# One instruction for the maxima of both attention maps of a block of queries

## What is computed

```python
h = rms_norm(x, norm_pre) * (1.0 + scale) + shift          # scale, shift, gate from c @ ada_w
q, k, v, z = (h @ w_in[:, i * 2048:(i + 1) * 2048] for i in range(4))
# 8 heads, two maps (m = 0, 1) of 128 features each, v of 256 features
for each block of 128 queries:
    sc = einsum('bqhmd,bkhmd->bhmqk', q, k) * scale
    p = softmax(where(mask, sc, NEG_INF))                  # causal by chunks of 64
    attn = p[:, :, 0] - lam * p[:, :, 1]
    o = attn @ v
o = rms_norm(o, subln) * 0.8 * silu(z)
out = x + gate * rms_norm(o @ w_out, norm_post)
```

## Time and profile before

| | us |
|---|---|
| median of three runs | 2067.22 (2063.76 to 2068.3) |
| the profiled execution | 2068.47 |
| its span | 2066.7 |
| busy: TensorE, VectorE, ScalarE, GpSimd | 1981.3, 1295.6, 785.1, 580.9 |
| seven heads beside the input products | about 826 to 1665 in the span |

### The profile page before, as it was taken

One profiled execution on the slowest core, in us unless ns is written; L12 is line 12 of the kernel. 1 busy time (PEld: TensorE's weight loads), 2 busy tenths in 40 slices (PEclk: granted clock), 3 DMA queues, 4 the chain that ended last, 5 costly groups with the idle time before them and its releaser, 6 DMA issues.

```text
span 2066.7 us, 26660 instructions
## 1 busy us (share of the span) xinstructions
PE 1981.3 (96%) x9324; PEld 1610.8 (78%) x9324; DVE 1295.6 (63%) x1988; ACT 785.1 (38%) x1567; POOL 580.9 (28%) x640
## 2 busy tenths in 40 slices
PE   3689999999999989999999999999999989999998
PEld 1168888888888878788888888888888878888886
DVE  3766676666566436777777777777777745434343
ACT  4333333333454323344444444444444333322240
POOL 2333233233456224232332333233232210000000
PEclk9889999999999999999999999999999999999999
DMA  9657666663556586776758676676767685476552
GB/s 311 198 183 244 221 199 207 200 197 124 175 183 227 211 325 219 207 236 195 233 178 248 196 216 216 209 236 200 234 193 237 196 275 165 123 229 199 178 153 82
DMA packets 391489, 426.52 MB, mean 206 GB/s; under 512 B 21078, under 2 KB 287420, under 8 KB 388796
## 3 DMA queue, kind: packets, MB, share of 16 engines
q1 hardware_dynamic: 391072, 424.76, 65.1%
q10 hardware_dynamic: 284, 0.05, 0.0%
HBM read 294.70 MB, written 130.03 MB: 206 GB/s over the span
## 4 chain that ended last, share of the span: by engine, by line
PE 90%; DMA 2%; DVE 2%; issue 2%; POOL 1%; ACT 1%; SPq 1%; DVEq 0%; POOLq 0%; ACTq 0%
PE ps L1561 28%; PE ps L1563 27%; PE ps L1562 27%; PE ps L1667 2%; PE ps L1675 2%; PE ps L1645 1%; DVE acc L1146 1%; PE ps L1541 1%; SPq L475 1%; PE ps L1694 1%; POOL sums L727 1%; POOL stg L747 1%; DMA h_dr<-stg 1%; DVE blk L1175 0%; DMA w_raw<-in_diff_w_out_dram 0%
## 5 line engine op out<-in xcount | busy, mean ns | idle before, releaser
L1561 PE MATMUL ps<-blk,ring 128*128 128x512 f32 x1536 | 612.4, 399 | 12.6 <-POOL blk L738 5.9
L1563 PE MATMUL ps<-blk,ring 128*128 128x512 f32 x1536 | 600.9, 391 | 0.0
L1562 PE MATMUL ps<-blk,ring 128*128 128x512 f32 x1536 | 600.4, 391 | 0.0
L1561 PEld LDWEIGHTS ps<-blk,ring 128*128 128x128 f32 x1536 | 289.7, 189 | 73.1 <-issue 12.1
L1563 PEld LDWEIGHTS ps<-blk,ring 128*128 128x128 f32 x1536 | 289.5, 188 | 62.2
L1562 PEld LDWEIGHTS ps<-blk,ring 128*128 128x128 f32 x1536 | 290.1, 189 | 57.2
L1111 DVE TENSOR_TENSOR ring<-sums,ring 128x512 fp32r<-128x512 f32 x256 | 221.1, 864 | 128.8 <-ACT ring L830 125.6
L727 POOL TENSOR_TENSOR sums<-raw 128x512 f32<-128x512 f32 x128 | 192.6, 1505 | 307.5 <-DVE ring L1111 290.4
L830 ACT ACTIVATE ring<-sums 128x512 fp32r<-128x512 f32 x256 | 160.4, 627 | 202.3 <-PE ps L1563 195.8
L1111 DVE TENSOR_TENSOR ring<-raw,ring 128x512 fp32r<-128x512 f32 x192 | 162.0, 845 | 83.0 <-ACT ring L830 82.3
L1432 DVE TENSOR_TENSOR w_lo<-w_raw,w_hi 128x512 fp32r<-128x512 f32 x112 | 77.4, 691 | 191.2 <-ACT w_hi L1026 191.1
(11 more groups left out here) (163 smaller groups left out, 3110.1 us busy)
## 6 DMA issues: line engine op xcount, KB each, us to landing
raw<-in_diff_w_in_dram SPq DMA_DIRECT2D x64, 1024.0 KB, 7.0
d_dr<-cc SPq DMA_DIRECT2D x128, 256.0 KB, 2.7
cc<-d_dr SPq DMA_DIRECT2D x128, 256.0 KB, 3.7
w_raw<-in_diff_w_out_dram SPq DMA_DIRECT2D x128, 256.0 KB, 3.6
ada<-in_ada_w_dram SPq DMA_DIRECT2D x108, 256.0 KB, 4.7
ada<-in_ada_w_dram SPq DMA_DIRECT2D x32, 512.0 KB
q_sb<-q_dr SPq DMA_DIRECT2D x64, 256.0 KB, 3.2
k_sb<-k_dr SPq DMA_DIRECT2D x64, 256.0 KB, 3.8
```

Source lines behind the costliest of these rows:

```text
L1561: MM(dst, a_hi, b_hi, start=start, stop=False, skip_group_check=True)
L1562: MM(dst, a_hi, b_lo, start=False, stop=False, skip_group_check=True)
L1563: return MM(dst, a_lo, b_hi, start=False, stop=stop, skip_group_check=True)
```

## The change

A new function `both_maxes` takes the place of the two calls of `maxes` for the heads 0 to 6. It waits for the scores of both maps, reduces all four banks seen as two maps of up to 1024 columns in one instruction with two results a partition, and raises `max_done` by two. `maxes` stays in use for the last head. Nothing else changes: ScalarE's `exps` still wait for `max_done` of one and of two.

```diff
--- before.py
+++ after.py
@@ -1302,6 +1302,14 @@
                 V.tensor_reduce(out=nmax[:, m:m + 1], in_=ps[:, bank:bank + 2].rearrange("p b n -> p (b n)")[:, 0:n],
                                 axis=AX.X, op=ALU.max, negate=True).then_inc(max_done, 1)
 
+            def both_maxes(h, qb):
+
+                a = h * NB + qb
+                n = (qb + 1) * P
+                dve.wait_ge(s_done, a * 2 + 2)
+                V.tensor_reduce(out=nmax[:, :], in_=ps[:, SC:SC + 4].rearrange("p (m b) n -> p m (b n)", m=2)[:, :, 0:n],
+                                axis=AX.X, op=ALU.max, negate=True).then_inc(max_done, 2)
+
             def out_scale(h, qb):
 
                 a = h * NB + qb
@@ -1362,8 +1370,7 @@
                 for qb in range(NB):
                     n0, n1 = SPREAD[qb]
                     a = (h - 1) * NB + qb
-                    maxes(h - 1, qb, 0)
-                    maxes(h - 1, qb, 1)
+                    both_maxes(h - 1, qb)
                     for i in range(n0):
                         weights(n)
                         if i == 0 and a:
```

## The result

The changed kernel takes 2087.39 us (median of six), the kernel before in the same comparison 2065.49. The ratio is 1.0101, with a 95% interval of 1.0083 to 1.0120: slower by 1.0%, about 21 us. One of the six executions stands apart, 2245.48 us at a granted clock of 0.846 instead of 0.987; the median holds it, the ratio leaves it out. The forecast was 26 us more and 2093 us, the range 2076 to 2101. The profiled execution has a span of 2084.8 us against 2066.7.

What follows compares the result with a forecast made beforehand. TensorE was taken to bound the seven-head stretch, so only later results could cost. Seven times the block terms, with qb 6 smaller in the last head, gave 26.0 us more, 2093 us on the median; range 2076 to 2101.

Steps and rivals of the forecast that it cites:

- What bounds the stage: Seven-head stretch: TensorE busy 834.78 of 839 us, so a VectorE change can only cost unless it shortens a TensorE wait.
- The rival by the other one: Whole kernel: VectorE's saved 8.8 us reach the end, giving 2058 us; chance of faster 0.02.
- the rival of the dearer instruction: All joint maxima: each costs two single ones, 5.5 us more, 2098 us; chance 0.09.
- The shift: Behind the exponentials: ScalarE free later by 0.133k + X, from 0.98 us at qb 2 to 2.18 at qb 7.
- qb 2: Block 2 of each head: `post_low` ends late, so TensorE's `v_turn` waits 0.47 us (0 to 0.6).
- qb 3: Block 3: GpSimd's third sum goes before `post_low`, `combine` ends late, and TensorE's `turn` starts 0.99 us later.
- qb 4: Block 4: the lower half `aT_low` starts 1.46 us later, costing TensorE 0.23 us (0 to 0.4).
- qb 5: Block 5: `aT_low` moves by 1.70 us, costing TensorE 0.39 us (0 to 0.5).
- qb 6: Block 6: late `cc_low` and GpSimd's next sum delay `combine`; TensorE waits 1.77 us, 0.77 in the last head.
- The reading of qb 3: Block 3, kernel before: third sum took 1.74 us and `post_low` 1.33, claimed as each waiting for the other.
- The signs: Joint maxima of 2.03 and 1.22 us, back-to-back exponentials, named TensorE waits, 3.8 us idle a head, heads 121 us.
- The rival of the meetings falling away: GpSimd meetings at blocks 3 and 6: VectorE moves to where GpSimd is idle, leaving 5.6 us, 2073; chance 0.10.

Runs made afterwards that it cites:

- the run with qb 6 alone: Kernel before with the joint maximum only in block qb 6, single maxima elsewhere: 2077.42 us against 2066.06, ratio 1.0058.
- the one with the free blocks: Kernel before with the joint maximum only in blocks qb 0, 1, 4, 5 and 7: 2068.72 us against 2066.06, ratio 1.0012.
- the last run: Joint maximum only in qb 0, 1, 4, 5 and 7, plus an unused second reduction at qb 7: 2077.74 us against the kernel before's 2066.04.
- the two runs with a sum moved: Changed kernel with GpSimd's first sum issued behind block qb 6: 2082.13 us; changed kernel with its third sum issued behind block qb 3: 2083.10 us.
- the run with `posts` ahead: Changed kernel with ScalarE's `posts` ahead of both exponentials in a block's first slot: 2068.31 us against the kernel before's 2066.04.
- one half of the change: Kernel before, both exponentials waiting for the second maximum: 2071.08 us; the other half, second maximum reading its banks twice, first one early: 2069.00 us.

## Why the prediction was right, point by point

**What bounds the stage.** Right. TensorE's busy time stayed, the stretch grew by its waits, and 8.8 us saved on VectorE had no effect. Of the two rules of the Trainium skill (Perfetto Trace Analysis, Optimizing Scalar/DVE Operations), the one on breaking up instructions is the one that the runs agree with. Its condition is that engines which aren't saturated cause bubbles on others; in the kernel before they caused none at these places, and the joining made them: 21 waits, 16.8 us. The rival by the other one (2058 us) is refuted.

**The joint maximum.** Its duration was right to 0.01 us at all lengths, so the rival of the dearer instruction falls. Its start was not: it does not come at the same moment as the second single one, but 0.07 us later in each of the 56 blocks (last section).

**The shift.** From the maximum's start, 0.95 measured at qb 2 for 0.98. With the 0.07 it is 1.02, and this is why qb 2 cost 0.55 and not 0.47.

**The sum, term by term** (a head, us; by the changed kernel's steps, with those of the single experiments where two places share a step):

```
place          worked out   measured
qb 2           0.47         0.55
qb 3           0.99         0.92
qb 4           0.23         0.10
qb 5           0.39         0.17  (0.06 at weighted, 0.12 in turn)
qb 6           1.77         1.58  (seventh head 0.77: 0.61)
qb 7           0            0.04  (the rest of turn at qb 6)
seven heads    26.0         22.1  (22.6 without the -0.5 of the loads)
```

The mechanism was right at each place but in `turn` of qb 5, and the total was 4 us too high. The 1.77 in the changed kernel's own row for qb 6 is the forecast number by chance, as it holds what was lost at qb 5. The two terms that were mis-sized are those of `aT_low`. At qb 4 I moved it by the whole 1.46 us; measured from the maximum's start it moved by 10.82 - 9.66 = 1.16, since small gaps in VectorE's queue in front of it were used up on the way. Its first piece then ended at 1259.35 + 0.68 = 1260.03, just in time. What is left, 0.10, is not idle time of TensorE but goes with a weight load that started late (below). At qb 5 it is the same: 11.06 - 9.69 = 1.37 us instead of 1.70, and `weighted` lost 0.06. The 0.12 in `turn` of qb 5 had no term at all in the forecast, though `combine` moves there by 1.68 us too, which with the 0.07 of the late start and the hand-over of 0.06 uses up its room of 1.78. The third is the hand-over: 0.14 is right for `v_turn`, but `turn` started 0.06 behind `combine` (1292.55 to 1292.61), which takes 0.08 each off qb 3 and qb 6. The remaining 0.1 at qb 6 is `combine`, 1.90 later where I had 2.07, with the 0.07 of the late start on the other side: 1.90 + 0.07, less a room of 0.44 - 0.06, is 1.59.

**The reading of qb 3.** The forecast read the two long durations of the kernel before as one meeting, `post_low` and the third sum waiting for each other. The third sum did wait for `post_low`, but `post_low` waited for the second sum. The term came out near its measurement (0.99 and 0.92) because who goes first in the changed kernel was read rightly.

**No carrying over from block to block.** Right: the run with qb 6 alone and the one with the free blocks add up, with the other blocks' terms, to the changed kernel's. It holds only where the block keeps some room: in the last run 0.31 us went on to the next block.

**The signs.** Joint maxima, exponentials back to back and the releasers came as said. TensorE's idle time is 2.4 us a head and not 3.8, and the heads went from 117.5 to 120.7 us and not to 121.

**The rival of the meetings falling away** (2073): its condition did not come about. No run shows its price of 5.6 us: with both sums moved and nothing else, if the two gains add up, 22.1 - 11.6 = 10.5 us would be left. What decided it was the argument that GpSimd's work moves with the same `ev`. By the two runs with a sum moved, taking these meetings away gives back 6 x 1.0 + 7 x 0.8 = 11.6 of the 22 us. This is no share beside the 19 us of the run with `posts` ahead; the two together are more than the whole, since at qb 3 and 6 either is enough to give back the same time. For the Trainium skill's rule (SBUF — State Buffer, SBUF: two separate sides), that whichever of the two starts first holds the shared port pair for the whole instruction (among others for an instruction of VectorE with two inputs in SBUF, against one of GpSimd that reads SBUF), the traces agree: 0.33 us decided at qb 3 who waited.

## What to carry to other kernels

An instruction that joins two others on an engine with time to spare saves its fixed part (0.157 us here) and costs the consumer the overlap of the first half: each step behind is later by the first result's own processing as well. So read not the busy share but the distance between each later result and the moment the bound engine asks for it, with everything that stands behind the delayed consumer in its queue; where that distance is larger than the shift, the edit is free. If the joint form is wanted, first put what others wait for ahead of the consumer. Here that made it free as far as the medians can tell, and still no gain.

## What was not expected of the hardware

**The joint maximum starts later.** In all 56 blocks it starts 0.43 us behind the start of the last matmul of the scores (at qb 3 1233.95 and 1234.38); the second single maximum of the kernel before started 0.36 behind it, in all 56 too (1225.02 and 1225.38). Neither the four banks nor the two results are the cause: the extra reduction in the last run has both and started 0.36 behind. What is the cause stays open.

**TensorE loses time before it idles.** At `weighted` of qb 4 the semaphore came 0.14 us before the matmul started, and the matmul started when it would have without any delay: 2.85 us after the first one behind `turn` in both kernels. But the weight load in front of it, which ran 0.23 us ahead in the kernel before (1250.27 and 1250.50), ran only 0.03 ahead (1260.14 and 1260.17), the matmul took 0.36 instead of 0.28, and the next followed after 0.20 instead of 0.11. The loss of about 0.1 us a head is in no idle time of the view of waits. That the late weight load makes it is a reading of these rows and was not tested by itself.

**Two small delays are not the sum of their costs.** With 0.05 us at qb 2 and 0.01 at qb 3 for one half of the change, and nothing for the other, both in one made 0.55 and 0.92.

**A chain can be reproduced to hundredths.** The same block made the same step within 0.03 us in six heads, the loads at qb 4 aside, and in kernels that differ elsewhere. Comparing the starts of one recurring instruction thus told 0.1 us a head, which the medians (intervals of 4 us and more) could not.
